# Two transformer blocks on one core: the last expert blocks by half tiles, gathered rows ahead of one-hots, stick scores multiplied once, the first norm shared by two engines

## The reference, cut to what matters

```python
xn = rms_norm(h, norm1_g)                      # first norm of all: tokens of x
proj = xn @ w_in; ...                          # block 1: HGRN2 and GLA heads, then w_out
h = h + peer_ffn(rms_norm(h), w_q, sub_keys, u, v)
mod = silu(c) @ ada_w + ada_b                  # block 2: modulation from c
...                                            # block 2: 8 retention heads, 8 stick heads
def stick_breaking(q, k, v):                   # z = q.k / sqrt(d), per head
    log_beta = log_sigmoid(z)
    log_stay = where(mask, log_beta - z, 0.0)
    log_w = log_beta + cumsum(log_stay, reverse=True) - log_stay
    return where(mask, exp(log_w), 0.0) @ v
def peer(xn, ...):                             # g: softmax of the 16 best pair scores
    act = gelu(xb . u[expert]) * g
    return sum(act * v[expert])                # added to h
```

## Time and profile before

| | us |
|---|---|
| median of three runs | 3253.9 |
| the profiled execution | 3244.14 |
| its span | 3242.3 |
| TensorE busy | 3074.7 (95%) |
| VectorE busy | 2404.8 (74%) |
| ScalarE busy | 1349.6 (42%) |
| GpSimd busy | 1296.6 (40%) |
| bytes moved by DMA | 931.22 MB, mean 287 GB/s |

### The profile page before, as it was taken

The page is one execution under the profiler, slowest core; times in us unless marked ns, Lnnn a source line. Parts: engine busy times, 40 slices in busy tenths (PEclk is TensorE's granted clock), DMA queues, the critical chain, the costliest instruction groups (busy, mean ns, idle before and its releaser), DMA issues. The chain is left out here.

```text
span 3242.3 us, 45915 instructions
## 1 busy us (share of the span) xinstructions
PE 3074.7 (95%) x16440; PEld 2049.9 (63%) x16440; DVE 2404.8 (74%) x5337; ACT 1349.6 (42%) x3424; POOL 1296.6 (40%) x1040
## 2 busy tenths in 40 slices
PE   6999899889999999999899999998999999999998
PEld 2466478766666666666344555687766666666664
DVE  5875449989899887877731243499899998888777
ACT  3232122686666555500211153125776655565100
POOL 0000000557665776666200000004576656676654
PEclk9999999999999999999999989999899999999999
DMA  8501251889999999999912011426999999999999
GB/s 300 195 27 52 98 208 63 322 308 409 409 408 389 407 409 409 409 409 409 353 59 84 17 56 39 178 83 245 332 384 409 409 398 403 409 409 409 409 409 358
DMA packets 282682, 931.22 MB, mean 287 GB/s; under 512 B 31804, under 2 KB 32460, under 8 KB 281944
## 3 DMA queue, kind: packets, MB, share of 16 engines
q0 software_dynamic: 147840, 536.96, 42.1%
q1 hardware_dynamic: 134616, 391.34, 31.9%
HBM read 921.87 MB, written 6.32 MB: 286 GB/s over the span
## 5 line engine op out<-in xcount | busy, mean ns | idle before, releaser
L763 PE MATMUL psum<-hT,mod 128*128 128x256 f32 x4096 | 962.5, 390 | 27.0 <-ACT big L1241 25.9
L763 PEld LDWEIGHTS psum<-hT,mod 128*128 128x128 f32 x4096 | 777.9, 194 | 147.8 <-issue 47.0
L1251 ACT ACTIVATE levels<-key_numbers,hT 128x128 bf16<-128x128 f32 x1792 | 566.6, 389 | 115.7 <-PE psum L801 115.6
L1959 DVE SCALAR_TENSOR_TENSOR tmp<-w,small,tmp 128x1024 f32<-128x1024 f32 x339 | 435.7, 1285 | 103.6 <-DMA w<-in_peer_v,tmp 50.1
L2129 POOL DMA_INDIRECT w<-in_peer_u,tmp x172 | 226.7, 1318 | 578.4 <-DVEq L1749 450.6
L1939 DVE CUSTOM_DVE_ANT_0 w<-w,hn 128x1024 f32<-128x1024 f32 x342 | 408.4, 1223 | 62.0 <-DMA w<-in_peer_down,tmp 30.9
L2129 POOL DMA_INDIRECT big<-in_peer_down,tmp x86 | 113.9, 1324 | 694.8 <-DVEq L1749 636.9
L773 PE MATMUL psum<-rows,big 128*128 128x512 f32 x768 | 343.9, 592 | 0.0
L801 PEld LDWEIGHTS psum<-x,levels 128*128 128x128 bf16 x6144 | 227.3, 103 | 148.2 <-issue 101.9
L1254 ACT ACTIVATE levels<-levels 128x512 bf16<-128x512 bf16 x448 | 282.2, 630 | 14.2
L2129 POOL DMA_INDIRECT w<-in_peer_down,tmp x170 | 224.7, 1322 | 139.7 <-DVE small L1939 99.9
(11 more groups left out here) (330 smaller groups left out, 4179.0 us busy)
## 6 DMA issues: line engine op xcount, KB each, us to landing
mod<-in_uT SPq DMA_DIRECT2D x256, 512.0 KB, 6.8
rows<-in_peer_v SPq DMA_DIRECT2D x64, 512.0 KB
rows<-in_peer_up SPq DMA_DIRECT2D x64, 512.0 KB
w<-in_w_in SPq DMA_DIRECT2D x14, 2048.0 KB, 8.4
srow<-in_peer_v SPq DMA_DIRECT2D x32, 512.0 KB
tmp<-in_peer_v SPq DMA_DIRECT2D x32, 512.0 KB, 6.8
srow<-in_peer_up SPq DMA_DIRECT2D x32, 512.0 KB
tmp<-in_peer_up SPq DMA_DIRECT2D x32, 512.0 KB, 7.0
```

What stands on the lines that cost most here:

```text
L763: last = nc.tensor.matmul(ps[4 + e % 2][:, 0:ND], ub[e % UV][:, k, :], hT[:, k, ND:SEQ], start=k == 0, stop=k == KC - 1)
L1251: last = nc.scalar.activation(hits[n % HITS][:, j * P:(j + 1) * P], keyno, ACT.Abs, bias=nibT[:, n * BATCH + j:n * BATCH + j + 1])
L1959: last = stt(y, row, c8[g % 2][:, b:b + 1], y, ALU.mult, ALU.add)
```

## The change

1. The last three blocks (`LAST = 3`) leave `second_product`. `last_products` multiplies them half tile by half tile, each half counted by `half_summed`; `finish_half` adds and `SP` stores each half (256 KB) by itself.
2. In `peer`, the units due for block e come before `first_keys` and the chooser's piece.
3. The second score matmul is gone. VectorE also writes min(z, 0) - ln to `ab` (four buffers instead of three), sums now leave out the key itself, and VectorE adds both into `st1`; ScalarE raises `st1` in place. The retention gating moves two steps later.
4. ScalarE loads the table of the square root at once and squares tiles 0 and 1; VectorE squares tiles 2 and 3. The loads of `c` and `hg_lower_logits` move ahead of `load_section(1)` and have a count of their own, `cond_in`.

```diff
-        "c_sticks": np.stack([-(j >= i).astype(np.float32), -np.ones((P, P), np.float32),
+        "c_sticks": np.stack([-(j > i).astype(np.float32), -np.ones((P, P), np.float32),
@@ SP
             load_section(0)
+                sp.dma_start(ccol[:, 0:KC], a["c_2"]...).then_inc(cond_in, 16)
+                sp.dma_start(lb3[:, 0:2, :], a["hg_lower_logits"]...).then_inc(cond_in, 16)
             load_section(1)
-                sp.dma_start(ccol[:, 0:KC], a["c_2"]...).then_inc(cst_in, 16)
-                sp.dma_start(lb3[:, 0:2, :], a["hg_lower_logits"]...).then_inc(cst_in, 16)
...
-            for t in range(NT):
+            for t in GATHERED:
                 sp.wait_ge(out_ready, t + 1)
                 sp.dma_start(out[t * P:(t + 1) * P, :], x[:, t, :]).then_inc(out_done, 16)
+            for n, t in enumerate(DENSE):
+                for c in range(2):
+                    cs = slice(c * SEC, (c + 1) * SEC)
+                    sp.wait_ge(out_ready, len(GATHERED) + 2 * n + c + 1)
+                    sp.dma_start(out[t * P:(t + 1) * P, cs], x[:, t, cs]).then_inc(out_done, 16)
@@ TensorE
+            def last_products(layer):
+                for n in range(len(DENSE)):
+                    for c in range(2):
+                        for e in range(NKEY - LAST, NKEY):
+                            pe.wait_ge(vb_in[e % UV], 16 * (at // UV + 1))
+                            pe.wait_ge(blk_ready, at + 1)
+                            last = nc.tensor.matmul(y_dense[n][:, c * 512:(c + 1) * 512], ...)
+                        if (n, c) == (1, 1):
+                            last.then_inc(blk_summed, LAST)
+                        else:
+                            last.then_inc(half_summed, 1)
...
-                        pe.wait_ge(w_exp, m - 1)
+                        pe.wait_ge(w_added, m - 1)
                     bank = ps[6 + m % 2]
-                    score(h, j, bank, True, False)
                     pe.wait_ge(sp_ready, m + 1)
-                    for i in range(NT - 1, j - 1, -1):
+                    for i in range(j, NT):
@@ ScalarE
+            nc.scalar.activation(std[:, 0:1], ones[:, 0:1], ACT.Sqrt)
-            for t in range(NT):
+            for t in range(2):
                 squares(t)
-            act.wait_ge(cst_in, 16 * 13)
+            act.wait_ge(cond_in, 16 * 2)
...
-                    act.wait_ge(ar_done, m + 1)
-                    nc.scalar.activation(st1[h % 2][:, j, j * P:SEQ], ps[6 + m % 2][:, 0:SEQ - j * P], ACT.Exp)
+                    act.wait_ge(w_added, m + 1)
+                    nc.scalar.activation(w, w, ACT.Exp).then_inc(w_exp, 1)
@@ VectorE
+            for t in (2, 3):
+                nc.vector.tensor_tensor_reduce(out=hn[:, t, :], in0=x[:, t, :], in1=x[:, t, :], ...)
...
+                    for n in range(units_due(e - 1), units_due(e)):
+                        run_unit(layer, n)
                     for m in range(spreads_due(e - 1), spreads_due(e)):
                         first_keys(1 + m // WIDES, m % WIDES)
                     for _ in range(pieces_due(e - 1), pieces_due(e)):
                         next(chooser)
-                    for n in range(units_due(e - 1), units_due(e)):
-                        run_unit(layer, n)
...
-                    finish_tile(layer, t, y_dense[n])
+                    for c in range(2):
+                        ...
+                        finish_half(layer, t, c, y_dense[n])
...
+                    tt(st1[h % 2][:, j, j * P:SEQ], ps[6 + m % 2][:, 0:wd], ab[m % (LOOK + 2)][:, 0:wd], ALU.add)
...
-                    stt(sv_, z_bank[...][:, 0:wd], 0.0, ab[...][:, 0:wd], ALU.max, ALU.add).then_inc(z_used, 1)
+                    stt(sv_, z, 0.0, l, ALU.max, ALU.add)
+                    stt(l, z, 0.0, l, ALU.min, ALU.subtract).then_inc(z_used, 1)
```

More of the change, by code:

```diff
@@ L38 @@
 WEIGHED = 4
+LAST = 3
 ZG = 20
@@ L335, in build @@
         t3 = part(tmp, 6, 2)
-        ab = [part(tmp, 2 * n, 2) for n in range(LOOK + 1)]
+        ab = [part(tmp, 2 * n, 2) for n in range(LOOK + 2)]
         z_bank = [ps[1], ps[4], ps[5]]
@@ L528, in _ @@
             load_section(0)
+            with nc.allow_non_contiguous_dma(reason="a few hundred values, one to a partition"):
+                sp.dma_start(ccol[:, 0:KC], a["c_2"].rearrange("(k p) -> p k", p=P)).then_inc(cond_in, 16)
+                sp.dma_start(lb3[:, 0:2, :], a["hg_lower_logits"].rearrange("r (h p) -> p r h", p=P)).then_inc(cond_in, 16)
             load_section(1)
             with nc.allow_non_contiguous_dma(reason="a few hundred values, one to a partition"):
-                sp.dma_start(ccol[:, 0:KC], a["c_2"].rearrange("(k p) -> p k", p=P)).then_inc(cst_in, 16)
-                sp.dma_start(lb3[:, 0:2, :], a["hg_lower_logits"].rearrange("r (h p) -> p r h", p=P)).then_inc(cst_in, 16)
                 sp.dma_start(bg, a["gla_b_gate"].rearrange("(h p) -> p h", p=P)).then_inc(cst_in, 16)
@@ L850, in _ @@
                 if i == 1:
-                    pe.wait_ge(cst_in, 16 * 13)
+                    pe.wait_ge(cst_in, 16 * 11)
                     for k in range(KC):
@@ L1073, in head_out @@
                 last.then_inc(pv_used, 1)
-            for t in range(NT):
+            seen.next(dve_to_act)
+            nc.scalar.activation(std[:, 0:1], ones[:, 0:1], ACT.Sqrt)
+            for t in range(2):
                 act.wait_ge(x_in, 16 * NT)
@@ L1459, in normed @@
                     normed_tile(t, gain, shift)
-            step(nc.vector.memset(ones, 1.0))
+            nc.vector.memset(ones, 1.0).then_inc(dve_to_act, 1)
+            for t in (2, 3):
+                dve.wait_ge(x_in, 16 * NT)
+                nc.vector.tensor_tensor_reduce(out=hn[:, t, :], in0=x[:, t, :], in1=x[:, t, :], scale=1.0, scalar=0.0,
+                                               op0=ALU.mult, op1=ALU.add, accum_out=ss[:, t:t + 1]).then_inc(ss_done, 1)
             dve.wait_ge(gain_in, 16)
@@ L1506, in _ @@
                 if n == 3:
+                    dve.wait_ge(cst_in, 16 * 11)
                     dve.wait_ge(low_done, 2)
@@ L1961, in add_rows, with finish_half @@
                     dve.wait_ge(v_free, n + 1)
+            def finish_half(layer, t, c, y):
+                cs = slice(c * SEC, (c + 1) * SEC)
+                if layer == 0:
+                    last = tt(x[:, t, cs], x[:, t, cs], y[:, cs], ALU.add)
+                    if c:
+                        last.then_inc(x_ready, 1)
+                        dve.wait_ge(x_ready, t + 1)
+                else:
+                    step(tt(ysum[:, cs], y[:, cs], rows[:, 2, cs], ALU.mult))
+                    tt(x[:, t, cs], x[:, t, cs], ysum[:, cs], ALU.add).then_inc(out_ready, 1)
             def finish_tile(layer, t, y):
-                if t in GATHERED:
-                    dve.wait_ge(gathered_x_back, 32 * (layer + 1))
+                dve.wait_ge(gathered_x_back, 32 * (layer + 1))
                 if layer == 0:
@@ L2058, in stick_squares @@
                                         stick_sq[h % 2].rearrange("p (t n) -> p t n", t=NT), AX_X, ALU.add).then_inc(heads_summed, 1)
-            for n in range(STICKS + LOOK):
+            for n in range(STICKS + LOOK + 1):
                 if n in (1, 4, 7, 10):
```

63 lines of the change are left out of this document (40 added, 23 removed).

## The result

| | before | changed | ratio, 95% |
|---|---|---|---|
| median of the runs, five of each | 3254.4 us | 3234.2 us (3227.5 to 3242.7) | 0.9924 (0.9902 to 0.9946) |
| changed kernel measured again (`again`) | 3256.8 | 3239.5 | 0.9943 (0.9922 to 0.9964) |
| the profiled executions | 3244.14 | 3242.71 | |

The change makes the kernel 0.6 to 0.8% faster, about 19 to 25 us (the two medians of the first row alone are 20 us apart); I had forecast 11.3. The two profiled executions differ by 1.4 us only. Neither is the usual one: before has its trace at 3244.14 while all its other executions, here and later, lie between 3247 and 3273 (but for one far outlier), and the trace of the changed kernel is its slowest of five.

The account below looks back on a forecast made before the run. TensorE was taken to pace the stick stage, TensorE and DMA both full in the steady expert stage. Terms -3.0 - 4.0 - 4.0 - 0.3 = -11.3 us gave 3242.6 as a median (3232.8 profiled); own range 3237 to 3248.

Parts of the forecast that it names:

- Start: Start of the modulation stage: reciprocal at 12.2 instead of 15.22, passed on through TensorE, -3.0 us (ends -4.5 and +1).
- the other sum that the prediction gave: Start: 1.9 us plus 2.66 for a table switch by the Trainium skill, some 4.5 us; not taken.
- Expert stages: Both layers' expert stages: gathers about 10 us earlier fill idle DMA, 2.0 us a layer, -4.0 (ends -18 and +8).
- The factor of 0.38: Expert stages: idle share of DMA, 15.3 of 40 us; four gathers' 5.2 us gain only this share, 2.0 us.
- Rival E: Expert stages: earlier gathers draw later ones, filling half of 15.3 us in each layer, 15.4; total 3231.2 us; chance 0.08.
- rival C: Stick and expert stages gain nothing: VectorE paces the one, late first keys or TensorE bind the other; 3250.6 us; chance 0.20.
- Stick stage: Stick stage: one score matmul a step removed, work added on VectorE, -4.0 us (ends -17.6 and +11).
- No gain in 5.5 heads: Stick stage, first 5.5 heads: VectorE's 11.3 us a head plus waits about as slow as TensorE's 11.75, nothing gained.
- 2.2 us a head: Stick stage: TensorE time removed per head, 17.6 us for eight; counted in the last 2.5 heads only, 5.6 us.
- The 1.6 us set against the gain for the clock: Stick stage: TensorE pauses more, so one third of a clock fall counted as loss, 1.6 us.
- rival D: Stick stage: TensorE's pauses bring three more clock falls, 18.6 us lost; whole kernel +9.7, 3263.6 us; chance 0.10.
- End: Kernel's end: last blocks added and stored by halves, last store 256 KB, -0.3 us (ends -3 and +0.6).

Follow-up runs that it names:

- its head: Kernel before plus the new order (units ahead of first keys and chooser pieces) in blocks 0 to 15 of each expert stage only: 0.9970 (0.9958 to 0.9982).
- before_2: The kernel before run once more for its trace, no edit, one execution: 3261.19 us.
- the later part of the order: Kernel before plus the new order in blocks 16 to 127 of each expert stage only: 0.9996 (0.9988 to 1.0005).
- stick_light: Kernel before plus the stick edit, retention heads centred and gated on 64 of 512 columns only, the rest left out: stick stage 93.0 us in its trace.

## Why the prediction was wrong

The sign and, within the intervals, the adding of stages were right; the size was 11.3 against 19 to 25 us, for two terms of the four were less than half of what they measure, and the profiled execution on which the sum was made was not a usual one.

- **Start, right.** 3.0 from the earlier trace rows was 2.9 in the trace from landing to reciprocal, the product near 32 came at 32.84, and alone it measures -3.9 (0 to -7.8). The 2.9 us are the sum made from the rows; the other sum that the prediction gave, some 4.5 us, did not come.
- **Expert stages, the step that failed.** I priced four gathers 10 us earlier at 5.2 us of DMA and then kept 0.38 of it, "they would have been moved later in that stretch in any case", and held TensorE's 0.98 for a second bound. The factor of 0.38 is what failed: in a stage of 977 us of transfers, with little idle behind the head, a byte moved into an idle gap leaves the end, as far as the traces tell, and gives its whole time. The term was 4.0; alone the order measures 10.7 and its head 9.8. 5.2 for each layer, unreduced, would have been 10.4, but that it comes so near is partly luck: the windows show 3.5 us for each layer, and some of these may be the second slow stretch, which was not in the rows at all. Rival E's mechanism (half of 15.3 us in each layer), at 0.08, was nearer for this term: 15.4. Beside it, came from an execution with 13.6 us of idle DMA in the head's 50 us where `before_2` has 17.7: there was more to fill than the rows showed.
- **The late first keys** that rival C named are there (5.96 and 3.70 us on TensorE), but the later part of the order costs nothing that can be told (-1.3, -3.9 to +1.6; its trace has waits of 6.2 and 6.4 us): the stage is bound by DMA, and the old order waits near there too. C gained nothing from them.
- **Stick stage, mis-sized in each term.** "No gain in 5.5 heads": from the first score to the fifth head's values were 77.0 us and are 72.4, 4.6 gained, for the stage opens 2.9 us sooner and the clock is at 0.50 for 20.4 us in place of 23.9. The retention work does set the pace there, as assumed (`stick_light`), but at heads 12.8 to 15.3 us apart, and before they had been 11.75, 16.3, 16.6 and 11.75: the 11.75 of the earlier trace rows, from late heads, was not what they all had. "2.2 us a head": removing the second scores took the distance from 11.75 to 10.23, 1.5 us, so the last three intervals gave 3.7 and not 5.6; for eight heads that is an estimated 12.2 at the range's end, not 17.6. The 1.6 us set against the gain for the clock had the wrong sign. Sum 8.3 in the traces, 9.1 (4.9 to 13.0) timed, 4.0 predicted. Of rival D the count came and the cost did not: the clock fell to 0.50 four times in the stage, near 1878, 1905, 1926 and 1936, instead of twice, but for 20.4 us in all instead of 23.9.
- **End.** 0.6 us less behind the last add in the trace; alone it measures -0.7 (-4.2 to +2.9), which cannot tell the 0.3 forecast from nothing.

## What to carry over

Ask first what a stage's length is made of: where the transfers' bytes over the steady rate, plus the idle of the DMA, give the length in every trace, an edit is priced by the idle it fills or makes, and a wait of TensorE only by the idle DMA that follows from it. Read the profile of the baseline against its own timed runs before making a sum on it; an execution 10 us faster than all of these lacks something that the usual ones have. Count what else changed in the window in which a gain is seen: here the slow stretch near 725 us went with the old order. And a cure that has a price of its own (the cap) does not tell what the ill cost.

## What the runs showed of the hardware

TensorE's instructions come by a DMA queue in packets of 16 KB, 256 to a packet (131 packets, 115 with 4096 instructions fewer). With batches of 96 short instructions and more than four gathers of 128 rows under way TensorE issued one to nine matmuls, with their weight loads, each 0.7 or 1.4 us for 3 to 12 us, and waited for nothing that the profile shows. A third of these matmuls, or a cap of four, removed it; half the bytes did not. That it runs short of instructions is the likeliest reading. How the gathers would hold up the packets stays open: the packets' own transfers took 0.9 to 2.3 us each, most of them about 1, and the packet came before, in or after the stretch. A cap of four gathers under way costs this kernel 4.2 to 4.6% (372 against 407 GB/s in its DMA-bound stage); one of six costs nothing that can be told (0.9927 with it, 0.9924 and 0.9943 without).
